# A bias-line store moved ahead of a weight load, and the pooling averages rewritten, in the opening of a one-core transformer kernel

## The reference, cut to what matters

```python
# x: (256, 1024), four groups of 256 channels, windows 2, 4, 8, 16
h = rmsnorm(x, norm_mixer[0])
for g, win in enumerate((2, 4, 8, 16)):
    cnt = min(t + 1, win)                         # tokens in the window
    d[g] = window_sum(h[g], win) / cnt - h[g]     # for each token t
x = x + einsum(d, pool_w) * pool_scale
x = x + swiglu(rmsnorm(x, norm_ffn[0]), w_gate_up[0], w_down[0])
# both attention layers later add a bias that depends on key distance alone:
# a row of values by distance for each of 16 + 8 heads ("the bias line")
# the second block is modulated by silu(c) @ ada_w + ada_b
```

## Time and profile before

| What | Value |
|---|---|
| median of three runs | 1399.37 us |
| the profiled execution | 1400.87 us |
| its span, first to last instruction | 1399.2 us |
| mean granted TensorE clock | 0.986 of full |
| PE, DVE, ACT, GpSimd busy | 95%, 48%, 37%, 14% of the span |
| first FFN product starts | 46.12 us into the span |

### The profile page before, as it was taken

The page is one execution under the profiler, slowest core; times in us unless marked ns, Lnnn a source line. Parts: engine busy times, 40 slices in busy tenths (PEclk is TensorE's granted clock), DMA queues, the critical chain, the costliest instruction groups (busy, mean ns, idle before and its releaser), DMA issues.

```text
span 1399.2 us, 24627 instructions
## 1 busy us (share of the span) xinstructions
PE 1330.1 (95%) x10580; PEld 1013.9 (72%) x10580; DVE 678.1 (48%) x1075; ACT 510.9 (37%) x829; POOL 197.9 (14%) x96
## 2 busy tenths in 40 slices
PE   5899999999999999999997889999999999999997
PEld 3899999988899999799895789744444444444433
DVE  6665665666666665788985443511121112212113
ACT  2433433556533333467454442222222222222212
POOL 0000000000000000376781663000000000000002
PEclk9999999999999999999999999999999999999999
DMA  9965455745455336452316035349999999999994
GB/s 370 408 271 185 176 185 217 302 130 215 168 182 188 148 123 231 193 215 96 138 46 271 3 118 225 122 193 423 423 426 426 423 428 426 422 428 424 422 426 174
DMA packets 37507, 363.43 MB, mean 260 GB/s; under 512 B 5027, under 2 KB 6179, under 8 KB 8740
## 3 DMA queue, kind: packets, MB, share of 16 engines
q1 hardware_dynamic: 36692, 359.56, 63.8%
q0 software_dynamic: 720, 2.46, 0.9%
HBM read 359.32 MB, written 2.69 MB: 259 GB/s over the span
## 4 chain that ended last, share of the span: by engine, by line
PE 82%; DVE 8%; ACT 3%; DMA 3%; POOL 2%; issue 1%; SPq 0%; DVEq 0%; POOLq 0%; ACTq 0%
PE banks L1289 16%; PE banks L715 13%; PE banks L717 13%; PE banks L716 13%; PE banks L1314 8%; PE banks L1240 4%; PE banks L1249 4%; DMA bias_line<-scr 2%; POOL slot_lo L627 2%; PE banks L693 1%; PE banks L704 1%; PE banks L1255 1%; DMA scr<-bias_line 1%; PE banks L1063 1%; DVE ring L2077 1%
## 5 line engine op out<-in xcount | busy, mean ns | idle before, releaser
L715 PE MATMUL banks<-h_hi,gu_hi 128*128 128x256 f32 x704 | 199.5, 283 | 0.0
L717 PE MATMUL banks<-h_hi,slot_lo 128*128 128x256 f32 x704 | 199.2, 283 | 0.0
L716 PE MATMUL banks<-h_lo,gu_hi 128*128 128x256 f32 x704 | 199.2, 283 | 0.0
L717 PE MATMUL banks<-slot_lo,slot_lo 128*128 128x256 f32 x480 | 136.3, 284 | 0.0
L715 PEld LDWEIGHTS banks<-h_hi,gu_hi 128*128 128x128 f32 x704 | 135.2, 192 | 0.7 <-DVE slot_lo L1759 0.5
L716 PEld LDWEIGHTS banks<-h_lo,gu_hi 128*128 128x128 f32 x704 | 135.2, 192 | 0.0
L717 PEld LDWEIGHTS banks<-h_hi,slot_lo 128*128 128x128 f32 x704 | 135.2, 192 | 0.0
L2313 DVE TENSOR_TENSOR out_lo<-banks,out_hi 128x512 fp32r<-128x512 f32 x62 | 42.9, 692 | 185.0 <-ACT out_hi L1701 185.0
L1314 PE MATMUL banks<-ring,scr 128*64 128x512 f32 x512 | 116.9, 598 | 1.9 <-ACT scr L1695 1.9
L1289 PE MATMUL banks<-ring,scr 128*64 128x512 f32 x512 | 112.6, 592 | 0.0
L1289 PE MATMUL banks<-ring 128*64 128x512 f32 x512 | 112.6, 592 | 0.0
(11 more groups left out here) (420 smaller groups left out, 2985.3 us busy)
## 6 DMA issues: line engine op xcount, KB each, us to landing
ring<-experts SPq DMA_DIRECT2D x64, 2048.0 KB, 10.9
ring<-ws SPq DMA_DIRECT2D x77, 1536.0 KB, 7.2
ring<-experts SPq DMA_DIRECT2D x64, 1024.0 KB, 11.0
ring<-ada SPq DMA_DIRECT2D x16, 1536.0 KB, 7.0
ring<-experts SPq DMA_DIRECT2D x1, 3072.0 KB, 10.1
scr<-bias_line POOLq DMA_DIRECT2D x4, 512.0 KB, 8.0
bias_line<-scr SPq DMA_DIRECT2D x1, 1536.0 KB
x<-xT SPq DMA_DIRECT2D x1, 1024.0 KB, 5.3
```

Of the source, the lines that this page charges most:

```text
L715: nc.tensor.matmul(out, hi, move_hi, start=start, stop=False, skip_group_check=True)
L716: nc.tensor.matmul(out, hi, move_lo, start=False, stop=False, skip_group_check=True)
L717: return nc.tensor.matmul(out, lo, move_hi, start=False, stop=stop, skip_group_check=True)
```

## The change

Three edits in the opening. (1) On SP the store of the bias line is issued before `load(0)` and the constants, directly behind modulation piece 3 and the wait for `line_copied`. (2) On ACT a dummy Sigmoid ahead of the wait for the vectors loads its table earlier, and the copy of the bias line moves behind the four squares. (3) The inverse counts cover the first 16 tokens alone (32 KB instead of 512 KB), and a group's averages take one multiplication of 2x16 columns, one fused multiply-and-subtract of 2x240 columns by the constant 1/window, and one subtraction of 2x16 columns.

```diff
+EARLY = 16
 def pool_inverse_counts():
-    t = np.arange(T)
+    t = np.arange(EARLY)
...
-        icnt, poolw = view(10880, 4, T), view(11904, 4, 2, T)
+        icnt, poolw = view(10880, 4, EARLY), view(11904, 4, 2, T)
...
             load_ada(3)
-            load(0)
             sp.wait_ge(line_copied, 1)
             heads = HEADS_1 + HEADS_2
+            sp.dma_start(bias_line, line_sb[0:heads, :].unsqueeze(1).broadcast_to([heads, SHIFTS, 2 * T])).then_inc(line_stored, 16)
+            load(0)
             sp.dma_start(con[:], consts).then_inc(const_loaded, 16)
-            sp.dma_start(bias_line, line_sb[0:heads, :].unsqueeze(1).broadcast_to([heads, SHIFTS, 2 * T])).then_inc(line_stored, 16)
...
+                if before_root is not None:      # in norm_squares, behind the squares
+                    before_root()
                 act.wait_ge(ss_ready, k + 1)
...
+            def copy_lines():
+                act.wait_ge(pe_step, 1)
+                nc.scalar.activation(line_sb[...], B[7][...], ACT.Copy).then_inc(line_copied, 1)
+
             act.wait_ge(ones_ready, 1)
+            nc.scalar.activation(small[:, 61:62], eps, ACT.Sigmoid)
             act.wait_ge(vec_loaded, 16)
             nc.scalar.activation(csig, ...)
             load_table(ACT.Sqrt)
-            act.wait_ge(pe_step, 1)
-            nc.scalar.activation(line_sb[...], B[7][...], ACT.Copy).then_inc(line_copied, 1)
-            norm_squares(0)
+            norm_squares(0, before_root=copy_lines)
...
-                then(nc.vector.tensor_tensor(hg, win, icnt[:, g:g + 1, :].broadcast_to([P, 2, T]), ALU.mult))
-                nc.vector.tensor_tensor(hg, hg, hp[:, 2 * g:2 * g + 2, PAD:], ALU.subtract).then_inc(pool_d, 1)
+                hg_0 = hp[:, 2 * g:2 * g + 2, PAD:]
+                nc.vector.tensor_tensor(hg[:, :, 0:EARLY], win[:, :, 0:EARLY], icnt[...], ALU.mult).then_inc(dve_step, 1)
+                nc.vector.scalar_tensor_tensor(hg[:, :, EARLY:], win[:, :, EARLY:], 1.0 / WINDOWS[g], hg_0[:, :, EARLY:], ALU.mult, ALU.subtract)
+                dve.wait_ge(dve_step, steps[0])
+                nc.vector.tensor_tensor(hg[:, :, 0:EARLY], hg[:, :, 0:EARLY], hg_0[:, :, 0:EARLY], ALU.subtract).then_inc(pool_d, 1)
```

More of the change, by code:

```diff
@@ L143, in pool_inverse_counts @@
 def pool_inverse_counts():
-    t = np.arange(T)
+    t = np.arange(EARLY)
     rows = [1.0 / np.minimum(t + 1, w).astype(np.float32) for w in WINDOWS]
-    return np.broadcast_to(np.stack(rows).astype(np.float32)[None], (P, 4, T)).copy()
+    return np.broadcast_to(np.stack(rows).astype(np.float32)[None], (P, 4, EARLY)).copy()
 def build(nc, xT, vec, consts, selector, inv_count, pool_w, ws, ada, rel, lora, router, router_bias, experts, final_row, out):
@@ L1350, in load_table, with norm_squares @@
                 nc.scalar.activation(small[:, 60:61], eps, func)
-            def norm_squares(k, weight=None, before_last=None):
+            def norm_squares(k, weight=None, before_last=None, before_root=None):
                 if k:
@@ L1419, in attention_steps @@
                 return exponentials, outputs, turned_weights
+            def copy_lines():
+                act.wait_ge(pe_step, 1)
+                nc.scalar.activation(line_sb[0:HEADS_1 + HEADS_2, :], B[7][0:HEADS_1 + HEADS_2, :], ACT.Copy).then_inc(line_copied, 1)
             act.wait_ge(ones_ready, 1)
+            nc.scalar.activation(small[:, 61:62], eps, ACT.Sigmoid)
             act.wait_ge(vec_loaded, 16)
@@ L1424, in _ @@
             load_table(ACT.Sqrt)
-            act.wait_ge(pe_step, 1)
-            nc.scalar.activation(line_sb[0:HEADS_1 + HEADS_2, :], B[7][0:HEADS_1 + HEADS_2, :], ACT.Copy).then_inc(line_copied, 1)
-            norm_squares(0)
+            norm_squares(0, before_root=copy_lines)
             act.wait_ge(pool_d, 4)
@@ L1877, in _ @@
                 hg = h[:, 2 * g:2 * g + 2, :]
-                then(nc.vector.tensor_tensor(hg, win, icnt[:, g:g + 1, :].broadcast_to([P, 2, T]), ALU.mult))
-                nc.vector.tensor_tensor(hg, hg, hp[:, 2 * g:2 * g + 2, PAD:], ALU.subtract).then_inc(pool_d, 1)
+                hg_0 = hp[:, 2 * g:2 * g + 2, PAD:]
+                nc.vector.tensor_tensor(hg[:, :, 0:EARLY], win[:, :, 0:EARLY], icnt[:, g:g + 1, :].broadcast_to([P, 2, EARLY]), ALU.mult).then_inc(dve_step, 1)
+                steps[0] += 1
+                nc.vector.scalar_tensor_tensor(hg[:, :, EARLY:], win[:, :, EARLY:], 1.0 / WINDOWS[g], hg_0[:, :, EARLY:], ALU.mult, ALU.subtract)
+                dve.wait_ge(dve_step, steps[0])
+                nc.vector.tensor_tensor(hg[:, :, 0:EARLY], hg[:, :, 0:EARLY], hg_0[:, :, 0:EARLY], ALU.subtract).then_inc(pool_d, 1)
             def pool_residual(g):
```

## The result

The changed kernel takes 1403.64 us, median of 7 runs, between 1399.31 and 1404.96. The kernel before, run beside it, takes 1400.01 (7 runs). The ratio is 1.0029, 95% interval 1.0017 to 1.0040, so the change costs 0.17 to 0.40%. The medians lie 3.6 us apart, and the ratio stands for 4.1 us, where 2.95 were forecast. The profiled execution takes 1402.63 us with a span of 1401.0.

What follows compares the result with a forecast made beforehand. PE, busy 95% of the span, bounds the kernel, so the first FFN product's start decides. The split ending at 41.75 instead of DVE's wait ending at 38.75 gave +2.95 us: 1399.37 to 1402.3, range 1397.9 to 1405.0.

Steps and rivals of the forecast that it cites:

- Piece 3: DMA queue: smaller counts save 1.1 us, so modulation piece 3 lands at 24.85 instead of 25.95.
- The line: DMA queue: the bias line's store takes 6.9 us behind piece 3, landing at 31.75, 7 us earlier.
- The slot behind it: DMA queue: `load(0)` takes 5.8 us behind the line, landing at 37.55, 7.9 us later than before.
- Behind the split: DVE to PE: from the split's end to the first FFN product, 7.37 us follow unchanged.
- Pooling: Pooling averages: four groups save 1.5 us, ending near 29.3; worth nothing while ACT waits for `load(0)`.
- ACT: ACT's opening: earlier Sigmoid table load and later line copy gain nothing; ACT still waits for x and PE's sums.
- SP held behind the store: SP: `load(0)`'s issue might take 19.31 us, until 30.4, still 1.3 us ahead of its turn.
- Rival (c): At ACT's `gu_hi`: `load(0)` overtakes the line, first product 5.2 us earlier, 1394.2 us; chance 0.06.
- rival (d): PE idles longer and its clock falls, 1.7 us more, 1404.0; or SP is held; chance together 0.10.
- Rival (a): DMA queue: the slot behind the line is clean; +0.9 to +2 us, about 1400.8; chance 0.22.
- one for one: Whole kernel: any shift of the first FFN product's start carries fully to the end; here +2.95 us.
- rival (b): DMA queue: the line itself takes 3.7 to 5 us; -2.3 to 0, about 1397.9; chance 0.12.

Runs made afterwards that it cites:

- x3: The changed kernel with slot 0 issued ahead of the line and the constants behind it; ratio 0.9977 to the kernel before (1395.74 us).
- x4: The changed kernel with the old SP order, the line in other columns, and ACT instead of DVE waiting for the store; ratio 0.9979 (1396.22 us).
- x1: The kernel before with the store's move alone, old pooling, ACT order and counts; ratio 1.0039 (1405.15 us).
- x7: The changed kernel with a line of 32 rows instead of 24, the added rows zeros; one profiled execution, 1399.94 us.
- x2: The changed kernel with SP's old order (slot 0, constants, line), so all edits but the store's move; ratio 0.9987 (1396.82 us).
- x8: The changed kernel profiled once more, nothing altered; one profiled execution, 1402.52 us.
- the two halves: The changed kernel, line in other columns, 16 copies stored ahead of slot 0 and 16 behind slot 1; one profiled execution, 1396.95 us.
- x9: The kernel of x4 with DVE's split of slot 0 ahead of pool residuals 0 and 1; ratio 0.9968 (1395.09 us).

## Why the prediction was right

- **Which transfer gates.** Forecast: the line's wait goes, slot 0's landing takes its place at `gu_hi`. The profile after shows just that, the move alone carries the loss, and two ways of taking slot 0 out from behind the line (x3, x4) turn it into a gain. Shown.
- **Piece 3** was to land at 24.85 and landed at 25.4. The counts did save their microsecond at the store's first packet (24.1 against 25.2 in x1), but the loads just ahead of the store ran slowly (below). In the five profiles where slot 0 or more stands between piece 3 and the store and the counts are small, piece 3 lands at 24.5 to 25.2.
- **The line** was given 6.9 us behind piece 3 and took 6.8: it landed at 32.13 where 31.75 were forecast, and what it is late is piece 3's.
- **The slot behind it** was given 5.8 us and took 5.9. In the other runs of this order it took between 4.7 and 6.0. The choice of the row of the same position over the clean 3.7 was what made the forecast come out right: with 3.7 the sum said +0.9. It was a choice of rows; the prediction did not work out why such a slot is slow, which the split of its engines (x7) shows in part.
- **Behind the split** 7.37 us were carried over. In the profile after it was 6.70 (42.25 to 48.95), and 6.4 where the last norm sums ran at the full clock (x1, x2, x8 and the second profile of the kernel before). So this term was 0.7 too large and made up for slot 0's half microsecond: 48.95 against 49.1. That the two came out so close is luck.
- **Pooling.** A group was costed at 1.09 us, or 1.0 if the small operations overlap. It takes 0.77, from one L1886 to the next. The three durations, 0.19, 0.65 and 0.18, were about right, but each starts 0.1 us before the one ahead has ended; the overlap was put too small. The four groups saved 2.2 us instead of 1.5. Still the pooling ended at 29.64 and not at 29.3, because the root of the norm came at 14.53 instead of 13.47. It is worth nothing in this order, as forecast.
- **ACT.** Nothing, as forecast: ACT idled 2.14 us for x at 7.55 and 4.31 for the norm's sums. These took 6.25 us on PE instead of 5.29, which is why the root came 1.06 us later; in the second profile of the kernel before, with ACT's old order, it came later still, at 14.82.
- **SP held behind the store**: the issue took 10.49 us, ended at 21.7 and cost nothing.
- **Rival (c)**, an overtaking slot 0, is out in five profiles of this order; in the four of them with 24 rows only the four engines that the line leaves free ran ahead. Of rival (d), the low stretch of the clock did come, 6.8 us long from 41 on, but in this profile it ended at 47.5, before the FFN began.
- **Rival (a),** a clean slot behind the line, is out too, but the two halves show when it would be right: behind 384 packets instead of 768.
- **What the sum left open.** The first product started 2.83 us later and the sum is right there, but the times of several executions differ by 3.6 to 4.1 us, and by 5.5 in x1. So the step "one for one" is not confirmed to the microsecond for the late orders; the runs do not show where the rest goes. For the faster orders it fits better: 3.1, 3.8 and 4.3 us at the first product in x3, x4 and x9, and 3.2, 2.9 and 4.5 by their ratios.
- **Two slips in its numbers,** neither of weight. 41.75 - 38.75 is +3.0, not +2.95. And rival (b) alone, a line of 3.7 to 5 us with the slot behind it still at 5.8, puts `load(0)` at 34.35 to 35.65, which is -0.2 to +1.1; its -2.3 needs a clean slot as well.

## What to carry to other kernels

A queue that is busy throughout has no early place to give: moving a transfer forward costs everything that it passes its whole length, and here also a slow transfer right behind it (5.9 us instead of 3.7). List what each transfer's first reader is and when that reader is ready for other reasons. Then put the one whose reader comes first in front: exchanging two neighbours took the ratio from 1.0029 to 0.9977 (x3), some 7 us. Where a wait only protects a buffer, look for other columns before reordering the queue; an edit nearby had just freed some.

## What the runs showed of the hardware that was not expected

- **A long run of 2 KB writes slows down in its second half.** By the trace's single packets the first 300 of the store's 768 take 84 ns each, and the last quarter takes 143 to 159 ns in the mean, in every profile with the whole store. Half the store alone stays at 84 to 86, and its second half, stored later, at 84 until its last packets. With 16 engines instead of 12 both rates rise by about a third (about 150 to 196 packets a us at first, 77 to 102 near the end), so the slowing belongs to the single engine's stream. It sets in about 3 us behind the first packet, after some 25 to 32 packets of an engine; the runs do not tell the time from the count, and why it sets in stays open.
- **Loads just ahead of the store are slow as well.** In the changed kernel the two microseconds before the store's first packet move 319 GB/s, with only loads running (the window's last columns are granted clock, DMA share and GB/s):

```profile
22.00:24.00 2.00, 2.00 (x16) 0.29 (x8) 1.97 (x2) 0.00 (x0) 0.00 (x0) 0.50 1.00 319
```

  The clean rate is 436. All 14 profiles have this, at 268 to 375 GB/s, whether the store stands behind a slot load or behind the constants, and the half store too. It fits piece 3's half microsecond. Whether it is the store's descriptors being fetched, or the reads of its source running ahead, was not tried.
- **SP is held at the issue behind the whole store.** It took 10.4 to 19.3 us in the 13 profiles with a whole store, and it ended 1.8 to 3.4 us before the store's first packet each time. Behind the first half of the line it took 0.41 us, behind the second 6.82. What sets the length is not shown.
- **TensorE's clock in the opening differs from run to run of one program.** PE is busy in bits there, and the stretch at 1.2 GHz that begins near 20 us was 3.4 us long in one profile of the kernel before and 13.6 in the other. This moves PE's pooling products between 7.1 and 10.2 us. Their length costs nothing while a transfer is the gate. In the faster orders x3, x4 and x9 they stand right in front of the path to the first product, at 9.8 to 10.0 us in each profile; what those orders would gain with 7.1 was not seen.
